# The first FFN of a fused layer in two phases: all up and gate tiles first, their product kept in DRAM, then the down projection in two halves

## The chip, the cores and the metric

One Trainium2 chip, one of its cores. The metric is the device time of one execution of the whole kernel in microseconds (us), median of several runs.

## The reference, cut to what matters

The layer works on 256 latent tokens and 256 context tokens of 2048 features, in float32. The context tokens go through the first FFN only as far as the mixer needs them.

```
def swiglu(u, w_in, w_out):                    # w_in 2048 x 11264, w_out 5632 x 2048
    gate, up = jnp.split(u @ w_in, 2, axis=-1)
    return (jax.nn.silu(gate) * up) @ w_out

ml = (jax.nn.silu(c) @ w_ada + b_ada).reshape(B, 9, D)       # modulation of the latents, 9 rows of 2048
mc = (jax.nn.silu(c_ctx)[None] @ w_ada + b_ada).reshape(1, 9, D)
h  = h  + 0.5 * ml[:, 2] * swiglu(modulate(rmsnorm(h,  g0), ml[:, 0], ml[:, 1]), ffn_w_in[0], ffn_w_out[0])
hc = hc + 0.5 * mc[:, 2] * swiglu(modulate(rmsnorm(hc, g0), mc[:, 0], mc[:, 1]), ffn_w_in[0], ffn_w_out[0])
# then: w_in projection of both streams, pooling and gated DeltaNet heads, w_out,
# a second FFN for the latents alone (ml[:, 6..8]), a final RMSNorm
```

## The kernel before, in words

Activations are held transposed, features on the 128 partitions and 512 tokens (both streams) along the free axis. Every float32 product is made of three matmuls (`product`, L744 to L748): each operand is split into a high part, rounded to the PE's fp32r format, and a low part, the remainder. A **weight tile** is 128 x 1024 floats. SyncE loads it into one of four `raw` buffers, ScalarE (ACT) casts it to its high part `wh` (L1419), VectorE (DVE) subtracts to get the low part `wl` (L1834), and TensorE (PE) uses it in 24 matmuls of 512 tokens. `wh` and `wl` are rings of four. ACT's cast of tile t waits on `tile_used`, until the PE is done with tile t-4. The split runs `AHEAD` = 3 tiles ahead of the PE, in program order: at step x of a group both ACT and DVE split tile x+3.

The first FFN is 11 groups of 512 hidden features. A group is 24 tiles (steps 0 to 23): 16 of up and gate weights (`UP_TILES`, two pairs of 8; each pair fills four PSUM banks) and 8 of the down projection. After the 8th and the 16th tile comes `hidden`: ACT applies silu to two banks (L1478), DVE multiplies (L2028), ACT casts to `hth` (L1481), DVE makes `htl` (L2032). The down projection of the group's four 128-row blocks follows at once, four output columns at a time, and DVE's `gate_out` multiplies it by the modulation gate and adds it to `h_lat` and `h_ctx` (L2050). Groups 0 and 1 are written out by hand: both groups' up tiles, then both groups' down tiles.

The modulation rows (silu(c) and silu(c_ctx) times `w_ada`) are made in two ways. Rows 0 and 1 (shift and scale) are made by the PE at the start. Row 2, the gates of this FFN, is made by the PE too, in 32 quarters (`gate_t`, L754, with L764) between the up tiles of groups 0 and 1. Rows 3 to 8 are made by DVE in **pieces** while the PE does the FFN. A piece has 16 items: ACT issues the load of 128 rows of `w_ada` into `abuf` (two buffers; 1024 columns in the first four pieces, 2048 in the last four; L1466 and L1470), and DVE multiplies them by the vector and adds them to `acc` (L2007, two instructions of 1024 columns for an item in both kinds). ACT's load of item i waits on `acc_done` until DVE has finished item i-2:

```
def load_piece(r, s, i, width):
    act.wait_ge(acc_done, steps(r, s, i - 1))
...
if width and 3 <= j < 3 + KT:            # ACT, step j, after the split of that step
    load_piece(r, s, j - 3, width)
...
if width and 5 <= j < 5 + KT:            # DVE, step j, after the split of that step
    piece(r, s, j - 5, width)
```

So both engines do a split and then the piece's part of that step, in the steps 3 to 18 (ACT) and 5 to 20 (DVE) of groups 2 to 9. The sums over the partitions are made by the PE in the next group (`reduce_rows`, L813, after its second tile, and `reduce_columns`, L820, after its fourth), eight times in all.

Of the kernel before, what the change touches and what calls it, by code (L numbers as in the profile page):

```python
# [11 lines left out]
ds = bass.ds  # L12
# [34 lines left out]
ADA_GATE = KT // 2  # L47
ADA_RING = 8
GATE_RING = 3
# [6 lines left out]
MOD_COLS = (N_MOD - 3) * KT  # L56
# [10 lines left out]
PIECE_FROM = 2  # L67
PIECE_BOTH = 4
PIECE_ONE = 4
LAST = GROUPS - 1  # L70
assert PIECE_FROM + PIECE_BOTH + PIECE_ONE == LAST

T_FFN1 = 0
T_HEADS = T_FFN1 + GROUPS * GROUP_TILES
# [3 lines left out]
T_END = T_FFN2 + GROUPS * GROUP_TILES  # L78


def transfers(t):

    if t < 2 * GROUP_TILES:
        return TILE_K if t < 2 * UP_TILES else 1
    if T_HEADS <= t < T_POOL:
        return TILE_K
    base = T_FFN1 if t < T_HEADS else T_FFN2
    inside = base <= t and (t - base) % GROUP_TILES < UP_TILES
    return TILE_K if inside else 1
# [4 lines left out]


GATE_HOOKS = ((2, 2, 2, 2, 2, 2, 0, 0), (2, 2, 2, 2, 2, 2, 0, 0), (0, 2, 2, 2, 2, 0, 0, 0))


def gate_steps():
    quarters, sums, m = [], [], 0  # L100
    for row in GATE_HOOKS:
        for n in row:
            done = [q // ADA_Q for q in quarters[-1] if q % ADA_Q == ADA_Q - 1] if quarters else []
            sums.append(done)
            quarters.append(list(range(m, m + n)))
            m += n
    assert m == ADA_GATE * ADA_Q
    return quarters, sums


GATE_QUARTERS, GATE_SUMS = gate_steps()
# [73 lines left out]
def laid_out(given):  # L185
# [4 lines left out]
    def columns(a):  # L190
# [5 lines left out]
    w = given["w_ada"][0, :, :3 * D].reshape(KT, P, 3, KT, P)  # L196
    first = w[:, :, 0:2].transpose(3, 0, 1, 2, 4).reshape(ADA_SS, KT, P, ADA_W)
    gate = w[:, :, 2].reshape(KT, P, ADA_GATE, ADA_W).transpose(2, 0, 1, 3)
    ada = np.concatenate([first, gate]).reshape(ADA_SS + ADA_GATE, ADA_Q, KT // ADA_Q, P, ADA_W)
    out = {"xT": features(given["x"]), "ctxT": features(given["ctx"]),  # L200
           "cols": np.ascontiguousarray(np.concatenate(cols + [host["tail"]], axis=1)),
           "ada": np.ascontiguousarray(ada.transpose(0, 1, 3, 2, 4).reshape(
               ADA_SS + ADA_GATE, ADA_Q, P, -1)),
# [12 lines left out]
def build(nc, xT, ctxT, cols_in, ada_in_w, masks_in, pools_in, w_out_t, w_ada, w_in, a_log, dt_bias,  # L216
# [11 lines left out]
    d_xp = scratch("d_xp", (HEADS, NBLK, 8, BLK, BLK))  # L228

    es = ExitStack()  # L230
    with es:  # L231
# [51 lines left out]
        with ExitStack() as st:  # L283
# [10 lines left out]
            with ExitStack() as first:  # L294
                ada_t = sb("ada_t", [P, ADA_RING, KT // ADA_Q, ADA_W], stack=first)
                gate_t = sb("gate_t", [P, GATE_RING, KT // ADA_Q, ADA_W], stack=first)
            with ExitStack() as later:
                sb("apart", [P, KT], stack=later)
                hth2 = sb("hth2", [P, GROUP_FF, SEQ], F32R, stack=later)
                htl2 = sb("htl2", [P, GROUP_FF, SEQ], F32R, stack=later)  # L300
            hth = sb("hth", [P, GROUP_FF, NTOK], F32R, stack=st)
            htl = sb("htl", [P, GROUP_FF, NTOK], F32R, stack=st)
            with ExitStack() as second:
                hth1 = sb("hth1", [P, GROUP_FF, NTOK], F32R, stack=second)
                htl1 = sb("htl1", [P, GROUP_FF, NTOK], F32R, stack=second)
            with ExitStack() as third:
                wba = sb("wba", [P, KT, N_BA], stack=third)
                wbah = sb("wbah", [P, KT, N_BA], F32R, stack=third)
                wbal = sb("wbal", [P, KT, N_BA], F32R, stack=third)
# [70 lines left out]
        gate_in = [sem(f"gate_in{i}") for i in range(GATE_RING)]  # L380
# [84 lines left out]
        STAT_BANK, RB_BANK = 5, (6, 7)  # L465
# [23 lines left out]
        def late_gates(k, s):  # L489

            return gates(0, 0, LAST, 0) + (2 * k + s + 1 if k < LATE else 2 * LATE + s * (KT - LATE) + k - LATE + 1)
# [5 lines left out]
        def steps(r, s, i):  # L497

            return r * (2 * KT) + ((s - PIECE_FROM) * 2 * KT + 2 * i + 4)

# [6 lines left out]
        def _(sp):  # L507
# [3 lines left out]
            for i in range(3):  # L511
                sp.sem_inc(gated[i], PER_DOWN[i])
# [31 lines left out]
            def first_load(t):  # L544
                if t < 2 * UP_TILES:
                    g, j = divmod(t, UP_TILES)
                    load(0, 0, t, up_source(0, 0, g, *divmod(j, K_TILES)))
                else:
                    g, j = divmod(t - 2 * UP_TILES, N_OUT * OUT_TILES)
                    load(0, 0, t, down_source(0, 0, g, *divmod(j, OUT_TILES)))  # L550
# [9 lines left out]
            def gate_load(m):  # L560
                if m >= GATE_RING:
                    sp.wait_ge(ada_used, ADA_SS * ADA_Q + m - GATE_RING + 1)
                sp.dma_start(gate_t[:, m % GATE_RING].rearrange("p k n -> p (k n)"),
                             ada_in_w[ADA_SS + m // ADA_Q, m % ADA_Q]).then_inc(gate_in[m % GATE_RING], 16)

            for i in range(ADA_SS):
                ada_load(i)
                if i >= 3:
                    first_load(i - 3)
            for t in range(13, 2 * GROUP_TILES):  # L570
                first_load(t)
                if t - 13 < len(GATE_QUARTERS):
                    for m in GATE_QUARTERS[t - 13]:
                        gate_load(m)
            with sp.Fori(0, GROUPS - 2) as r:
                group_loads(0, r, 2, 2 * GROUP_TILES)
# [164 lines left out]
        def _(pe):  # L741
            mm, turn = nc.tensor.matmul, nc.tensor.transpose

            def product(out, ah, al, bh, bl, first, last):  # L744

                mm(out, ah, bh, start=first, stop=False)  # L746
                mm(out, ah, bl, start=False, stop=False)  # L747
                return mm(out, al, bh, start=False, stop=last)  # L748
# [59 lines left out]
            def reduce_rows():  # L808


                for c_ in range(4):
                    s, half = divmod(c_, 2)
                    i = mm(ps[32 * c_:32 * (c_ + 1), 7, :], ones.broadcast_to([P, 32]),  # L813
                           acc[:, s, half * TILE_N:(half + 1) * TILE_N], start=True, stop=True)
                i.then_inc(red_pe, 1)

            def reduce_columns():

                for b in range(4):
                    i = mm(ps[:, 7, b:16:4], rsum[:, b * P:(b + 1) * P], sel4, start=True, stop=True)  # L820
# [10 lines left out]
            def up_tile(f, r, t, p, k, x_base=None):  # L831

                pe.wait_ge(lo_done, tiles(r, GROUP_TILES, t) + RAW)
# [36 lines left out]
            def last_block(t):  # L870


                def part(q, kk, bank, x_):
                    k, a = divmod(kk, TILE_K)
                    w = slice(a * TILE_N + q * P, a * TILE_N + (q + 1) * P)
                    return product(ps[:, bank, 0:SEQ], wh[:, (t + k) % HL, w], wl[:, (t + k) % HL, w],
                                   hth[:, kk, x_], htl[:, kk, x_], kk == 0, kk == GROUP_FF - 1)

                pe.wait_ge(lo_done, tiles(0, GROUP_TILES, t + OUT_TILES - 1) + RAW)
                for q in range(4):  # L880
                    for kk in range(GROUP_FF):
                        i = part(q, kk, 4 + q, slice(0, SEQ))
                    i.then_inc(down_done[0], 1)
                pe.wait_ge(gated[0], gates(0, 0, LAST, 3))
                for q in range(4):
                    for kk in range(GROUP_FF):
                        i = part(q, kk, CTX_BANK[q], slice(SEQ, NTOK))
                        if q == 3 and kk % TILE_K == TILE_K - 1:
                            i.then_inc(tile_used, 1)
                    if q < 3:  # L890
                        i.then_inc(down_done[0], 1)
                    if q == 0:
                        stream_sums(0)
                    elif q == 1:
                        stream_rms(0)

            def first_groups():
# [27 lines left out]
                for pair in range(1, 2 * PAIRS):  # L925
                    free = 0 if pair % 2 else 4
                    if pair == 1:
                        pe.wait_ge(cols_set, ADA_SS)
                    else:
                        pe.wait_ge(F[0]["hf_done"], 2 * (pair - 1))  # L930
                        pe.wait_ge(cols_set, ADA_SS + 3 * (pair - 1))
                    for k in range(K_TILES):
                        up_tile(0, 0, pair * K_TILES + k, pair % 2, k)
                        hook = (pair - 1) * K_TILES + k
                        for m in GATE_QUARTERS[hook]:
                            j, q = divmod(m, ADA_Q)
                            if q == 0:
                                pe.wait_ge(F[0]["hf_done"], 2 * pair)
                                pe.wait_ge(arow_set, ADA_SS + j - 1)
# [1713 lines left out]
```

## Time and profile before

| | |
|---|---|
| median of 3 runs | 2919.83 us (2917.42 to 2921.59) |
| span of the profiled execution, first to last instruction | 2915.5 us |
| the profiled execution's own time | not listed apart; the runs' median is 4.3 us above the span |
| PE busy (matmuls) | 2855.9 us, 98% |
| DVE busy | 1687.6 us, 58% |
| ACT busy | 968.1 us, 33% |
| mean DMA rate | 186 GB/s |

A busy share is that of the whole span. Matmuls overlap each other in the records, so the mean duration of one is not its cost; the distance from one start to the next is. The first FFN lies between 65 and 1578 us, the heads and the mixer up to about 2150, the second FFN after that.

### The profile page before, as it was taken

How to read it: one execution, taken by the hardware profiler on the slowest of the kernel's cores; microseconds unless marked ns; L12 is line 12 of the kernel's file. 1: busy time of each engine (PE TensorE's matmuls, PEld its weight loads, DVE VectorE, ACT ScalarE, POOL GpSimd, SP SyncE). 2: the span in 40 equal slices, each digit the busy share in tenths (PEclk: the TensorE clock that was granted, in tenths of full speed). 3: DMA queues.
4: the chain of work that ended last, by engine and by line, in shares of the span. 5: the costliest groups of instructions: out<-in, count | busy, mean ns of one | idle time of the engine just before them, and what ended most of it. 6: DMA issues, size and time to landing. Idle time of an engine off the chain costs nothing. (4 is left out here: it accounts for less than half of the span.)

```text
span 2915.5 us, 47677 instructions
## 1 busy us (share of the span) xinstructions
PE 2855.9 (98%) x18096; PEld 2492.1 (85%) x18096; DVE 1687.6 (58%) x2472; ACT 968.1 (33%) x1443; POOL 238.5 (8%) x388
## 2 busy tenths in 40 slices
PE   6999999999999999999999999999999999999998
PEld 3677888888888888888888888878999999999998
DVE  2522547475665757575726766755675555555555
ACT  2212222222222222222224555544353344344444
POOL 3000000000000000000002013545120000000001
PEclk9999999999999999999999999999999999999999
DMA  9865245555455857567632566685556666566664
GB/s 362 295 208 168 88 144 173 153 155 169 144 173 155 269 185 254 193 224 231 196 98 77 153 194 188 196 260 173 159 178 190 187 184 184 180 186 187 187 187 144
DMA packets 399198, 541.70 MB, mean 186 GB/s; under 512 B 51040, under 2 KB 301920, under 8 KB 390384
## 3 DMA queue, kind: packets, MB, share of 16 engines
q1 hardware_dynamic: 377408, 434.20, 48.4%
q10 hardware_dynamic: 21680, 106.03, 11.1%
q8 instruction: 70, 1.15, 0.2%
q14 instruction: 40, 0.33, 0.0%
HBM read 518.08 MB, written 22.05 MB: 185 GB/s over the span
## 5 line engine op out<-in xcount | busy, mean ns | idle before, releaser
L1834 DVE TENSOR_TENSOR wl<-raw,wh 128x1024 fp32r<-128x1024 f32 x640 | 782.5, 1232 | 722.7 <-ACT wh L1419 721.0
L1419 ACT CAST wh<-raw 128x1024 fp32r<-128x1024 f32 x640 | 666.1, 1047 | 1506.2 <-PE ps L748 1142.5
L746 PE MATMUL ps<-xh,wh 128*128 128x512 f32 (+1 forms) x1920 | 729.8, 380 | 3.2 <-DVE xl L1894 2.5
L747 PE MATMUL ps<-xl,wh 128*128 128x512 f32 (+1 forms) x1920 | 722.2, 376 | 0.0
L748 PE MATMUL ps<-xh,wl 128*128 128x512 f32 (+1 forms) x1920 | 721.5, 376 | 0.0
L748 PE MATMUL ps<-hth,wl 128*128 128x256 f32 (+1 forms) x1424 | 473.8, 333 | 0.0
L746 PE MATMUL ps<-hth,wh 128*128 128x256 f32 (+1 forms) x1424 | 473.3, 332 | 0.0
L747 PE MATMUL ps<-htl,wh 128*128 128x256 f32 (+1 forms) x1424 | 473.1, 332 | 0.0
L746 PEld LDWEIGHTS ps<-xh,wh 128*128 128x128 f32 x1920 | 361.6, 188 | 80.9 <-issue 11.2
L748 PEld LDWEIGHTS ps<-xh,wl 128*128 128x128 f32 x1920 | 361.3, 188 | 67.3
L747 PEld LDWEIGHTS ps<-xl,wh 128*128 128x128 f32 x1920 | 361.7, 188 | 64.9
L746 PE MATMUL ps<-x2h,wh 128*128 128x256 f32 x1408 | 393.8, 280 | 1.7 <-DVE x2l L1894 1.7
L748 PE MATMUL ps<-x2h,wl 128*128 128x256 f32 x1408 | 395.0, 281 | 0.0
L747 PE MATMUL ps<-x2l,wh 128*128 128x256 f32 x1408 | 393.6, 280 | 0.0
L2007 DVE SCALAR_TENSOR_TENSOR acc<-abuf,cT,acc 128x1024 f32<-128x1024 f32 x240 | 297.1, 1280 | 0.2 <-DMA abuf<-in_w_ada 0.2
L747 PEld LDWEIGHTS ps<-htl,wh 128*128 128x128 f32 x1424 | 267.6, 188 | 26.7
L748 PEld LDWEIGHTS ps<-hth,wl 128*128 128x128 f32 x1424 | 267.4, 188 | 26.9
L746 PEld LDWEIGHTS ps<-hth,wh 128*128 128x128 f32 x1424 | 266.9, 187 | 27.3
L746 PEld LDWEIGHTS ps<-x2h,wh 128*128 128x128 f32 x1408 | 264.2, 188 | 2.0 <-issue 2.0
L747 PEld LDWEIGHTS ps<-x2l,wh 128*128 128x128 f32 x1408 | 265.6, 189 | 0.0
L748 PEld LDWEIGHTS ps<-x2h,wl 128*128 128x128 f32 x1408 | 265.1, 188 | 0.0
L2480 POOL TENSOR_TENSOR nacc<-hf 128x512 f32<-128x512 f32 (+1 forms) x4 | 5.4, 1359 | 2232.3 <-ACT hf L1509 1486.9
(264 smaller groups left out, 2287.8 us busy)
## 6 DMA issues: line engine op xcount, KB each, us to landing
raw<-in_ffn_w_in SPq DMA_DIRECT2D x704, 256.0 KB, 3.3
raw<-in_ffn_w_out SPq DMA_DIRECT2D x176, 512.0 KB, 4.1
abuf<-in_w_ada ACTq DMA_DIRECT2D x64, 1024.0 KB, 5.8
ada_t<-in_ada SPq DMA_DIRECT2D x64, 512.0 KB, 9.3
abuf<-in_w_ada ACTq DMA_DIRECT2D x64, 512.0 KB, 3.8
raw<-in_w_in SPq DMA_DIRECT2D x128, 256.0 KB, 3.7
gate_t<-in_ada SPq DMA_DIRECT2D x32, 512.0 KB, 5.0
raw<-in_w_out SPq DMA_DIRECT2D x32, 512.0 KB, 4.6
```

The source lines that it names most:

```text
L746: mm(out, ah, bh, start=first, stop=False)
L747: mm(out, ah, bl, start=False, stop=False)
L748: return mm(out, al, bh, start=False, stop=last)
L1419: nc.scalar.copy(wh[:, t % HL, :], raw[:, t % RAW, :]).then_inc(hi_done, 1)
L1834: tt(wl[:, t % HL, :], raw[:, t % RAW, :], wh[:, t % HL, :].bitcast(F32), ALU.subtract).then_inc(lo_done, 1)
L2007: n = stt(acc[:, b, :], src, c_, acc[:, b, :], ALU.mult, ALU.add)
L2480: i = tt(nacc[:, x_], sq[:, 0, x_], sq[:, 1, x_], ALU.add)
```

## The change

The first FFN becomes two phases. In the **up phase** all 11 groups of 16 up and gate tiles follow one another (`up_pairs`). The product of each pair, high and low part, is written to a DRAM tensor `d_h` by two DMAs of ACT (`hidden_out`), at step 10 of the same group for the first pair and at step 2 of the next for the second. The last group's four blocks stay in SBUF. In the **down phase** the output is made in two halves of 1024 features. A half runs over all 44 blocks, one weight tile of 128 x 1024 for each, into all eight PSUM banks, and adds to `h_lat` and `h_ctx` once at its end. ACT loads the blocks from 5 on back (`hidden_in`, 512 KB each) into the upper rows of `xl`. A half is closed bank by bank over its last tiles: 2 in the first half, 4 in the second, whose last four output blocks are closed for the latents and then the context, as before.

The gates (row 2) are no longer made by the PE's quarters. They are two further pieces, so there are 10: six of 1024 columns for both streams, then four of 2048. Item i of a piece is loaded at step i+10 of its group or step i-6 of the next, and worked on by DVE at step i+12 or i-4. The sums are made by the PE after tile 11 and after tile 13 of the next group.

```diff
-PIECE_BOTH = 4
-PIECE_ONE = 4
+PIECE_BOTH = 3 * D // HALF                       # 6
+PIECE_ONE = (N_MOD - 5) * D // (2 * HALF)        # 4
+PIECE_AT = 12
+LOAD_AT = PIECE_AT - 2
+K_FF = D_FF // P                                 # 44
+HELD = 2 * PAIRS                                 # 4
+SPILLED = GROUPS * PAIRS - PAIRS
+HALF_TILES = K_FF
+CLOSE = 2
+CLOSE_LAST = 4
+HR = 4
...
# TensorE
-            def reduce_rows():
+            def reduce_rows(r, n):
+                pe.wait_ge(acc_done, steps(r, n, KT))
+                pe.wait_ge(F[0]["hf_done"], r * GROUP_FF + ((n + 1) * GROUP_FF + 2))
...
-                        for m in GATE_QUARTERS[hook]:
-                            j, q = divmod(m, ADA_Q)
...
-                            ada_quarter(q, free + j % 2, gate_t[:, m % GATE_RING],
-                                        gate_in[m % GATE_RING], 16 * (m // GATE_RING + 1))
-                        for j in GATE_SUMS[hook]:
-                            ada_columns(ADA_SS + j, free + 2)
...
+            def up_pairs(r, m):
+                for x in range(UP_TILES):
+                    p, k = divmod(x, K_TILES)
+                    if k == 0:
+                        pe.wait_ge(F[0]["hf_done"], r * GROUP_FF + (m * GROUP_FF + 2 * p - 2))
+                        if p == 0 and m >= 2:
+                            pe.wait_ge(red_out, r * 2 + 2 * (m - 1))
+                    up_tile(0, r, m * UP_TILES + x, p, k)
+                    if x == PIECE_AT - 1:
+                        reduce_rows(r, m - 1)
+                    elif x == PIECE_AT + 1:
+                        reduce_columns(r, m - 1)
...
+            def down():
...
+                for a, close in enumerate((CLOSE, CLOSE_LAST)):
+                    for i in range(HELD):
+                        ff_tile(0, a, i)
+                    with pe.Fori(0, (HALF_TILES - HELD) // HR - 1) as r:
+                        for b in range(HR):
+                            ff_tile(r, a, HELD + b)
+                    for i in range(HALF_TILES - HR, HALF_TILES - close):
+                        ff_tile(0, a, i)
+                    closing_tiles = range(HALF_TILES - close, HALF_TILES)
+                    for i in closing_tiles:
+                        ff_arrived(0, a, i)
+                    for c in range(8 if a == 0 else 4):
+                        ff_whole(a, c, closing_tiles)
...
# ScalarE
+            def up_pairs(r, m, before=None):
+                for x in range(UP_TILES):
...
+                    split(r, UP_TILES, m * UP_TILES + x + AHEAD)
+                    if x < LOAD_AT and m:
+                        load_piece(r, m - 1, x + KT - LOAD_AT)
+                    elif x >= LOAD_AT and m < GROUPS - 1:
+                        load_piece(r, m, x - LOAD_AT)
+                    if x == 2 and m:
+                        hidden_out(r, m, -1)
+                    elif x == K_TILES + 2 and m < GROUPS - 1:
+                        hidden_out(r, m, 0)
+                    if x % K_TILES == K_TILES - 1:
...
+                        hidden(0, r, m, tiles(r, UP_TILES, m * UP_TILES + x), p, hth)
+
+            def down_tile(r, a, i, spread=True):
+                split(r, HR, T_DOWN + a * HALF_TILES + i + AHEAD)
+                if HELD <= i + AHEAD and spread:
+                    hidden_in(r, a, i + AHEAD)
...
# VectorE
+            def up_pairs(r, m):
+                for x in range(UP_TILES):
+                    if m or x >= K_TILES - 1:
+                        split(r, UP_TILES, m * UP_TILES + x + AHEAD)
+                    if m and x == PIECE_AT:
+                        reduced_rows(r, m - 1)
+                    elif m and x == PIECE_AT + 2:
+                        reduced(r, m - 1)
+                    if x < PIECE_AT and m:
+                        piece(r, m - 1, x + KT - PIECE_AT)
+                    elif x >= PIECE_AT and m < GROUPS - 1:
+                        piece(r, m, x - PIECE_AT)
+                    if x % K_TILES == K_TILES - 1:
+                        hidden(0, r, m, x // K_TILES, hth, htl)
```

Two places show how instructions move. The first is ACT at the start of a group of the loop over the wide pieces. Before, it holds splits alone up to step 3:

```order
L1418 ISA
L1419 CAST wh<-raw 128x1024
L1417 REGISTER_ALU
L1418 REGISTER_ALU
L1419 CAST wh<-raw 128x1024
L1418 REGISTER_ALU
L1419 CAST wh<-raw 128x1024
L1418 REGISTER_ALU
L1419 CAST wh<-raw 128x1024
L1463 ISA
L1470 ISA
L1470 DMA abuf<-in_w_ada 128x2048
```

The same place after the change, from the group's third split on:

```order
L1455 CAST wh<-raw 128x1024
L1500 REGISTER_ALU
L1506 ISA
L1506 DMA abuf<-in_w_ada 128x2048
L1531 ISA
L1534 ISA
L1534 DMA d_h<-hth 128x2x512
L1534 ISA
L1534 DMA d_h<-htl 128x2x512
L1454 REGISTER_ALU
L1455 CAST wh<-raw 128x1024
```

Each split is now followed by the load of an item, in every step, and in step 2 (and 10) by the two stores of a pair as well.

The second is the PE at the first sum of a piece. Before, it stands after two tiles of the group, whose predecessor's items ended at step 20:

```order
L748 MATMUL ps<-xh,wl 128x512
L964 REGISTER_ALU
L965 REGISTER_ALU
L813 MATMUL ps<-acc,cols 32x512 x4
L833 REGISTER_ALU
L746 MATMUL ps<-xh,wh 128x512
```

After the change it stands between tile 11 and tile 12 of the group, and DVE's last item of that piece is at step 11:

```order
L758 MATMUL ps<-xh,wh 128x512
L759 MATMUL ps<-xl,wh 128x512
L760 MATMUL ps<-xh,wl 128x512
L826 MATMUL ps<-acc,cols 32x512 x4
L758 MATMUL ps<-xh,wh 128x512
```

The sum moved from five steps behind the last item to the end of the tile in whose time the last item is worked on.

## Rows read from the trace of the kernel before

**Rows 1.** The page: busy time, and the span in 40 slices (tenths)

```profile
PE 2855.9 (98%) x18096; PEld 2492.1 (85%) x18096; DVE 1687.6 (58%) x2472; ACT 968.1 (33%) x1443; POOL 238.5 (8%) x388
...
PE   6999999999999999999999999999999999999998
...
PEclk9999999999999999999999999999999999999999
```

**Rows 2.** Groups: count | busy us, mean ns | idle before, releasers

```profile
L746 PE MATMUL ps<-xh,wh 128*128 128x512 f32 (+1 forms) x1920 | 729.8, 380 | 3.2 <-DVE xl L1894 2.5
```

**Rows 3.** Windows of PE: length, busy (instructions), granted clock, DMA share, GB/s

```profile
131.84:294.94 163.10, 163.10 (x906) 1.00 0.58 187
...
381.98:469.02 87.04, 87.04 (x386) 1.00 0.57 169
512.54:601.75 89.21, 89.21 (x401) 1.00 0.56 165
```

**Rows 4.** Windows of all engines (PE, PEld, DVE, ACT, POOL), steps 8 to 14

```profile
1089.00:1127.00 38.00, 38.00 (x169) 31.49 (x168) 26.25 (x24) 9.55 (x11) 0.00 (x0) 1.00 0.84 279
```

**Rows 5.** Timeline of PE, then ACT: start, duration, steps 6 to 8

```profile
1083.78 0.39 PE L746 MATMUL ps<-xh,wh 128*128 128x512 f32 x1
...
1078.54 1.05 ACT L1419 CAST wh<-raw 128x1024 fp32r<-128x1024 f32 x1 [4.39 <-PE ps L748]
...
1083.98 1.05 ACT L1419 CAST wh<-raw 128x1024 fp32r<-128x1024 f32 x1 [4.39 <-PE ps L748]
...
1089.42 1.09 ACT L1478 ACTIVATE sg<-ps 128x512 f32<-128x512 f32 x2 [4.39 <-PE ps L748]
1090.77 1.22 ACT L1481 CAST hth<-hf 128x512 fp32r<-128x512 f32 x2 [0.27 <-DVE hf L2028]
1091.89 1.04 ACT L1419 CAST wh<-raw 128x1024 fp32r<-128x1024 f32 x1
```

**Rows 6.** Timeline of ACT, then DVE, steps 10 and 11

```profile
1102.13 0.34 ACTq L1470 DMA_DIRECT2D abuf<-in_w_ada  x1
1102.60 1.05 ACT L1419 CAST wh<-raw 128x1024 fp32r<-128x1024 f32 x1 [4.28 <-DVE acc L2007]
1107.45 0.34 ACTq L1470 DMA_DIRECT2D abuf<-in_w_ada  x1
1107.92 1.05 ACT L1419 CAST wh<-raw 128x1024 fp32r<-128x1024 f32 x1 [4.27 <-DVE acc L2007]
...
1103.68 1.22 DVE L1834 TENSOR_TENSOR wl<-raw,wh 128x1024 fp32r<-128x1024 f32 x1 [1.71 <-ACT wh L1419]
1104.82 2.47 DVE L2007 SCALAR_TENSOR_TENSOR acc<-abuf,cT,acc 128x1024 f32<-128x1024 f32 x2
```

**Rows 7.** Timeline of ACT, steps 15 and 16

```profile
1129.27 1.05 ACT L1419 CAST wh<-raw 128x1024 fp32r<-128x1024 f32 x1 [4.27 <-DVE acc L2007]
...
1134.59 1.09 ACT L1478 ACTIVATE sg<-ps 128x512 f32<-128x512 f32 x2 [4.27 <-DVE acc L2007]
...
1137.07 1.04 ACT L1419 CAST wh<-raw 128x1024 fp32r<-128x1024 f32 x1
```

**Rows 8.** Lines L1466 (512 KB) and L1470 (1 MB): from issue to landing

```profile
DMA to landing us min/median/max: 3.5/3.8/5.1
...
DMA to landing us min/median/max: 4.7/5.8/8.4
```

**Rows 9.** Timeline of PE around two stretches of lower clock, and one as window

```profile
1951.20 0.63 PE L1200 MATMUL ps<-GI,UF 32*32 32x32 f32 x16 [3.04 <-DMA UF<-d_uf]
...
1951.00:1961.00 10.00, 9.74 (x118) 0.50 1.05 383
...
126.78 0.77 PE L746 MATMUL ps<-xh,wh 128*128 128x512 f32 x1
...
131.62 0.39 PE L748 MATMUL ps<-xh,wl 128*128 128x512 f32 x1
```

More of the change, by code:

```diff
@@ L55 @@
 PB = HALF // P
-MOD_COLS = (N_MOD - 3) * KT
+MOD_COLS = (N_MOD - 2) * KT
+M_GATE, M_SHIFT1, M_SCALE1, M_GATE1, M_SHIFT2, M_SCALE2, M_GATE2 = (KT * i for i in range(N_MOD - 2))
 GROUP_FF = 4
@@ L78 @@
 T_END = T_FFN2 + GROUPS * GROUP_TILES
+SPARE = (T_HEADS, T_HEADS + 1)
 def transfers(t):
-    if t < 2 * GROUP_TILES:
-        return TILE_K if t < 2 * UP_TILES else 1
-    if T_HEADS <= t < T_POOL:
-        return TILE_K
-    base = T_FFN1 if t < T_HEADS else T_FFN2
-    inside = base <= t and (t - base) % GROUP_TILES < UP_TILES
+    if t < T_DOWN:
+        return TILE_K
+    if t < T_HEADS:
+        return 1
+    if t < T_POOL:
+        return TILE_K
+    inside = T_FFN2 <= t and (t - T_FFN2) % GROUP_TILES < UP_TILES
     return TILE_K if inside else 1
 FIRST_TILES = {6: 0, 7: 1, 8: 2, 9: 3, 11: 4, 13: 5, 15: 6}
[L96 to L111, printed above, removed]
 SCAN = ((2, 3, 0, 1), (3, 2, 1, 0))
@@ L510, in _ @@
             sp.sem_inc(tile_used, HL)
-            for i in range(3):
+            for i in range(1, 3):
                 sp.sem_inc(gated[i], PER_DOWN[i])
@@ L742, in _, with product @@
             mm, turn = nc.tensor.matmul, nc.tensor.transpose
[L744 to L748, printed above, removed]
+            def product(out, ah, al, bh, bl, first, last, reopened=False):
+                mm(out, ah, bh, start=first, stop=False, skip_group_check=reopened)
+                mm(out, ah, bl, start=False, stop=False, skip_group_check=reopened)
+                return mm(out, al, bh, start=False, stop=last, skip_group_check=reopened)
             def ada_quarter(q, bank, buf, arrived, count):
@@ L868, in down_block, with ff_part @@
                             mark(part(q, kk), q, kk)
[L870 to L892, printed above, removed]
+            def ff_part(a, i, c, x_, last=False, reopened=False):
+                t = T_DOWN + a * HALF_TILES + i
+                w = slice(c * P, (c + 1) * P)
+                bh, bl = held(i) if i < HELD else fetched(i)
+                return product(ps[:, down_bank(a, c), x_], wh[:, t % HL, w], wl[:, t % HL, w], bh[:, x_], bl[:, x_],
+                               i == 0, last, reopened)
@@ new lines, in hidden_out, with hidden_in @@
+            def hidden_out(r, m, p):
+                n, b = 2 * m + p, 2 * (p % 2)
+                act.wait_ge(F[0]["h_ready"], r * GROUP_FF + 2 * (n + 1))
+                rows = slice(2 * n, 2 * n + 2) if isinstance(r, int) else ds(r * GROUP_FF + 2 * n, 2)
+                for part, src in enumerate((hth, htl)):
+                    act.dma_start(d_h[rows, :, part, :].rearrange("b p n -> p b n"), src[:, b:b + 2, :].bitcast(F32)
+                                  ).then_inc(hid_out, 16)
+            def hidden_in(r, a, i):
+                rows = slice(i - HELD, i - HELD + 1) if isinstance(r, int) else ds(r * HR + i - HELD, 1)
+                at_ = 8 + 2 * (i % HR)
+                act.dma_start(xl[:, at_:at_ + 2, :].bitcast(F32), d_h[rows].rearrange("b p s n -> p (b s) n")
+                              ).then_inc(hid_in[i % HR], 16)
@@ L1747, in _, with first_high @@
                 split(0, 0, t)
-            for t in range(2 * GROUP_TILES):
-                if t < K_TILES:
-                    high(0, 2 * t)
-                    high(0, 2 * t + 1)
-                split(0, 0, t + AHEAD)
-                if t < 2 * UP_TILES and t % K_TILES == K_TILES - 1:
-                    g, p = divmod(t // K_TILES, PAIRS)
-                    hidden(0, 0, g, t + 1, p, (hth, hth1)[g])
-            with act.Fori(0, PIECE_BOTH) as r:
-                group(0, r, PIECE_FROM, PIECE_FROM * GROUP_TILES, width=1)
-            with act.Fori(0, PIECE_ONE) as r:
-                s = PIECE_FROM + PIECE_BOTH
-                group(0, r, s, s * GROUP_TILES, width=2)
-            group(0, 0, LAST, LAST * GROUP_TILES, closing=last_squares, early=decay_weights, left=1)
+            def first_high(x):
+                if x < K_TILES:
+                    high(0, 2 * x)
+                    high(0, 2 * x + 1)
+            up_pairs(0, 0, first_high)
+            with act.Fori(0, PIECE_BOTH - 1) as r:
+                up_pairs(r, 1)
+            up_pairs(0, PIECE_BOTH)
+            with act.Fori(0, PIECE_ONE - 1) as r:
+                up_pairs(r, PIECE_BOTH + 1)
+            up_pairs(0, GROUPS - 1)
+            down()
             square_stream(LATE, 1)
```

398 lines of the change are left out of this document (214 added, 184 removed).

## Prediction

> **What bounds the kernel now.** I read the page first [rows 1]: the PE is busy for 98% of the span, slice after slice of the first FFN is full and its clock stays high there. The groups of instructions give the same for the PE's idle time: ahead of the FFN tiles' first matmul form there are 3.2 us in 1920 instructions [rows 2]. So the time is now what the PE's program costs, and work of other engines is free as long as it is in time. The windows give the PE's prices [rows 3]. Sixteen up tiles of a group without a sum take 87.04 us, 5.44 us for a tile. With one piece's two sums among them they take 89.21, so the two sums of a piece cost 2.17 us. The stretch with the PE's quarters of row 2 is 163.10 us long.
>
> Next I read who works beside the PE while a piece is made. Between 1089 and 1127 us DVE is busy for 26.25 of 38 us and ACT for 9.55 [rows 4]; by share neither is near its limit. The timelines show another thing. ACT's cast starts 0.20 us after the PE's tile starts (1083.78, 1083.98) when it is on time [rows 5]. With an item in each step it is not the PE that releases ACT but DVE: the idle time before the cast ends with "DVE acc L2007" [rows 6]. Cast, subtraction, the item's two instructions, the issue of the next load: cast to cast is 1102.60 to 1107.92, 5.32 us. The PE's step is 5.44, so a delayed chain gains only 0.12 us in a step. The item of a step ends at 1104.82 + 2.47 = 1107.29, that is 4.69 us after its cast began.
>
> **What is removed.** The 163.10 us hold 612 product matmuls of the FFN, 25.5 tiles, 138.7 us at 5.44. The rest is 24.4; a column sum of another row within it, about 0.4, stays. Gates: **-24.0 us**. The FFN's products themselves are the same in number (24 matmuls for each of 264 tiles).
>
> **What is added on the PE.** Two more pieces are summed: 2 x 2.17 = **+4.3 us**.
>
> **The wait at the first sum.** The PE's first sum now stands behind tile 11 and needs item 15, which DVE works on in step 11, in the time of that very tile. Before, items ended at step 20 and the sum came five steps later, so a delay of the chain reached nobody. Now the margin is what is left of one tile: 5.44 - 0.20 - 4.69 = 0.55 us when the chain is on time. It is not on time. One passage of `hidden` takes ACT from cast to cast 1083.98 to 1091.89, 7.91 us, so it costs 2.47 over a tile [rows 5]; inside a late chain 1129.27 to 1137.07, 7.80, so 2.36 [rows 7]. Both passages of a group (steps 15 and 7) now lie between one sum and the next with an item in every step; before, eight or so steps of a group had no item, in which the delay was paid back. Then `hidden_out`: two stores in step 2 and two in step 10, issued by ACT right between the load and the next cast. An issue shifts ACT's next cast by 0.47 us (1102.13 to 1102.60) [rows 6], four of them 1.88. About ten steps pay back 0.12 each, 1.2. The delay at step 11 is 2.47 + 2.36 + 1.88 - 1.2 = 5.5 us; less the margin, the PE waits 5.0 us in a group. DVE's two copies of sums are paid by the PE's own 2.17 us beside them. Nine groups make 45; in the last group the stores of step 10 and the loads after it are missing, so some 2.2. **+47.2 us.** The bounds: without the stores in the chain it is 3.1 a group, about 28 in all; if an issue that stands behind another DMA took twice as long, about 64.
>
> The Trainium skill ("DMA: Bandwidth & Descriptors", section "Issuing engines are not separate DMA queues") says that the time an engine's sequencer takes to initiate a DMA is usually small beside the DMA itself. The trace agrees on the size, 0.47 us against landings of 3.8 and 5.8 us [rows 6, 8]. By that rule one would price the stores at nothing and get about 19 us less.
>
> **The clock after the wait.** The PE has not stood still in this FFN so far, so the price comes from two other places [rows 9]. After a wait of 3.04 us the stretch from 1951 to 1961 ran at a granted clock of 0.50, the lower level, 1.2 GHz. From 126.78 to 131.62, after short waits of about 0.6 us among light matmuls, eleven starts took 4.84 us, where 11 x 0.2267 = 2.49 is the full pace: 2.3 us lost. I take 2.3 us for each of ten waits, **+23 us**. Bounds: nothing, if the clock stays up through 5 us of standing still, and about 4 us for a wait (+40), if the lower level holds as in the first of the two places.
>
> **The DMA beside the wide pieces.** Steps 8 to 14 of a wide piece already have the DMA engines busy for 0.84 of the time at 279 GB/s [rows 4]; in proportion, 332 GB/s is the full rate. A group with a wide piece now moves 16 x 0.5 MB of weights, 16 x 1 MB of `w_ada` and 1 MB of stores with both parts, 27.3 million bytes. Over 87.04 + 2.17 + 5.0 = 94.2 us that is 290 GB/s, 0.87: it fits on average. But a load of `abuf` is issued when the item two before is done and is wanted about 7.7 us later, and such a load lands after 4.7 to 8.4 us, median 5.8 [rows 8]. Late ones delay the chain that already ends the PE's wait. I put 1 us for each of four groups, **+4 us**; bounds 0 and 3 us a group.
>
> **The down phase.** In a tile of 5.44 us ACT casts for 1.05 and issues one load, DVE subtracts for 1.23 [rows 6]: no chain comes near. `hidden_in` is issued three tiles ahead, some 14 us, and 512 KB land after 3.8 us, at most 5.1 [rows 8]. Closing the first half over two tiles gives DVE one bank per six matmuls, 1.36 us, for an addition of 512 columns; an item's 2 x 1024 columns take it 2.47 [rows 6], so I estimate a bank at some 0.7 us and this closing at nothing (bounds 0 and 3 us, were each bank late by a third). In the second half the last four tiles are held until all four are there, and there are only four `wh`: the cast and the load of block 43 start when tile 39 has been used. That is 0.2 for ACT's start, 0.2 for issues and 3.8 for the landing [rows 8], **+4.0 us**, and another 2.3 for the clock. These two are **+6.3**. If tile 43's block were issued earlier than the cast, this falls to about nothing; if its load lands late, 5.6.
>
> **The sum.** -24.0 + 4.3 + 47.2 + 23 + 4 + 6.3 = +60.8. On the profiled execution's span of 2915.5 this gives 2976.3; the median is 4.3 us above the span, so 2980.6, rounded to **2980 us**.
>
> **The rivals.** A: *the PE's sum decides, no wait.* Spoken for by the shares in [rows 4], where DVE has a third of its time free; against it stands the cast-to-cast distance of 5.32 in [rows 6]. The time would be -24.0 + 4.3 + 4 = -15.7, so 2904. It decides if the wait at the first sum stays under about 1 us a group with the clock up, that is, if the chain runs at some 4.9 us a step so that passages are paid back in five steps. This is the other sign: faster. Chance 0.07. The Trainium skill ("Perfetto Trace Analysis", section "Identifying the Most-Contended Engine") tells one to find the limiting engine by occupancy; by it DVE is no limit and the PE's own work decides. That row agrees on the shares, and the rule leaves out the order in which the items must come.
>
> B: *the same wait at the lower size.* The stores' issues lie outside the chain (28 instead of 47.2), and the clock stays up or nearly: -24.0 + 4.3 + 28 + 4 + 4 = +16.3, 2936; with a third of the clock's price, 2944. For it: the clock's price comes from places with lighter matmuls before the wait. Chance 0.12.
>
> C: *the wide pieces become DMA-bound.* Every item's 1 MB lands late because the stores share the queues with loads at 0.84 busy. With 20 to 30 us more for the four wide groups the time is 3005 to 3015 and above. Against it: the rate needed, 290 GB/s, lies below 332. Chance 0.06.
>
> My forecast has the remaining 0.75.
>
> **How the numbers follow.** The likeliest case alone reaches from 2951 (no clock price, nothing for the DMA: 60.8 - 25.3 - 4 = +31.5) to 3005 (12 for the DMA, 17 more for the clock: +85.8, rounded). Eight times in ten the range should hold the time; it takes in the upper half of B, and the lower part of C: 2938 to 3010. A measurement of this kernel can tell about 0.2%, 6 us, from no change. Faster by more than that: rival A and a rest of other mishaps in my prices, 0.08. Within: 0.02, since it would need the waits to sum to just the gates' 20 us. Slower: 0.90.
>
> **What would show it.** In the changed kernel the PE's timeline has, in front of the sum's matmuls behind tile 11 of each group from the second on, an idle time of 4 to 6 us ended by DVE's `acc`, ten in all; a group period near 96 us instead of 89.2; a granted clock below 1 in the window behind that sum and near 1 elsewhere; no such gap in the down phase until the last four tiles, where one of some 4 us is ended by a cast or by a landing. ACT's casts in the up phase are released by DVE's items from step to step. It would be wrong if those gaps are under 1 us (A), if the gaps are 3 us and the clock doesn't fall (B), or if DVE's items wait for a DMA (C).

## The result, and the profile after

The changed kernel takes 2977.14 us (median of 4 runs, 2968.99 to 2980.93) against 2918.62 us for the kernel before (4 runs, 2913.81 to 2921.59). The ratio is 1.0201, 95% interval 1.018 to 1.0221: slower by 58.5 us. The forecast was 2980 and slower. Single runs of one kernel spread by some 10 us, and part of that lies where no edit of this document reaches: from the sums of the norm ahead of it to those of the last norm, the second FFN lasts 745.1 and 745.3 us in the traces of experiments 3 and 4 and 754.0 to 754.5 us in the other nine.

The page of the kernel after answers to [rows 1]: the PE has 256 matmuls fewer and DVE is less busy than before, ACT is where it was, yet the PE's share fell from 98 to 96%. The slices show hardly more (one dip in the first FFN, one later): waits of 6 us are too short for slices of 74. The mean clock stands in the row of the core, 0.977; the trace of the kernel before has 0.994, and the kernel of experiment 1 below, which has hardly any of the waits, 0.989.

```profile
PE 2858.0 (96%) x17840; PEld 2496.2 (84%) x17840; DVE 1633.4 (55%) x2197; ACT 968.1 (33%) x1443; POOL 237.9 (8%) x388
...
PE   6999999999998999999999999998999999999998
```

```profile
core 0: 2978.0 us, clock 0.977
```

So the page says "less work, and slower". The timeline of the PE shows where the time is. This is the sum behind tile 11 of the fifth group (start, duration, engine, line, operation, idle time before it and what ended it):

```profile
539.89 0.39 PE L760 MATMUL ps<-xh,wl 128*128 128x512 f32 x1
546.17 1.93 PE L826 MATMUL ps<-acc,cols 128*32 128x512 f32 x8 [5.89 <-DVE acc L2092]
```

There are ten such waits, as forecast, of 6.05, 5.90, 5.91, 5.89, 5.89, 3.41, 6.78, 7.45, 5.82 and 3.14 us. The windows put a price on one group (length, PE busy, granted clock, DMA share, GB/s): from sum to sum in the narrow pieces, in the sixth, in a wide piece, then the wait alone and the 9.83 us behind it.

```profile
448.28:546.17 97.89, 92.00 (x401) 0.95 0.63 193
642.95:738.28 95.33, 91.92 (x401) 0.97 0.64 194
837.08:936.67 99.59, 92.14 (x400) 0.95 0.81 274
540.27:546.17 5.90, 0.01 (x2) 0.72 0.93 292
546.17:556.00 9.83, 9.83 (x40) 0.82 0.68 212
```

A group took 89.21 us of the PE before [rows 3]; the first one shown takes 97.89. The chain ahead of the wait is to be read on ACT, which answers to [rows 5 to 7]: two steps, one with the stores.

```profile
529.55 1.05 ACT L1455 CAST wh<-raw 128x1024 fp32r<-128x1024 f32 x1 [4.33 <-PE ps L760]
534.41 0.34 ACTq L1503 DMA_DIRECT2D abuf<-in_w_ada  x1
534.87 1.05 ACT L1455 CAST wh<-raw 128x1024 fp32r<-128x1024 f32 x1 [4.27 <-PE ps L760]
539.73 0.34 ACTq L1503 DMA_DIRECT2D abuf<-in_w_ada  x1
540.24 0.41 ACTq L1534 DMA_DIRECT2D d_h<-hth  x1
540.81 0.41 ACTq L1534 DMA_DIRECT2D d_h<-htl  x1
541.34 1.04 ACT L1455 CAST wh<-raw 128x1024 fp32r<-128x1024 f32 x1 [5.42 <-issue]
```

529.55 to 534.87 is 5.32, the step forecast. 534.87 to 541.34 is 6.47: the two stores shift the next cast by 1.15 us. (The releaser "PE ps L760" is the row's inference for a cast that follows a load; the load at 534.41 comes 0.17 us behind DVE's item, which ends at 534.24.) The last wait of the down phase is there too:

```profile
1608.89 0.39 PE L760 MATMUL ps<-xl,wl 128*128 128x512 f32 x1
1612.87 0.76 PE L758 MATMUL ps<-xl,wh 128*128 128x512 f32 x1 [3.59 <-DVE el L1929]
```

### The profile page after: what moved, and what is told of

Read it like the earlier page. It is cut to its first block and busy times, and to the rows that moved or that the text cites. A ratio compares the mean times of both kernels' runs of the same rounds, so it can differ in the third digit from the quotient of the medians.

```text
span 2978.0 us, 47625 instructions
## 1 busy us (share of the span) xinstructions
PE 2858.0 (96%) x17840; PEld 2496.2 (84%) x17840; DVE 1633.4 (55%) x2197; ACT 968.1 (33%) x1443; POOL 237.9 (8%) x388
## 5 line engine op out<-in xcount | busy, mean ns | idle before, releaser
L759 PE MATMUL ps<-xl,wh 128*128 128x512 f32 (+1 forms) x2560 | 973.8, 380 | 0.0
L760 PE MATMUL ps<-xh,wl 128*128 128x512 f32 (+1 forms) x1904 | 720.8, 379 | 0.0
L759 PEld LDWEIGHTS ps<-xl,wh 128*128 128x128 f32 x2560 | 485.9, 190 | 90.8
L760 PEld LDWEIGHTS ps<-xh,wl 128*128 128x128 f32 x1904 | 361.2, 190 | 67.4
L760 PE MATMUL ps<-x2h,wl 128*128 128x256 f32 x1408 | 393.8, 280 | 0.0
L2092 DVE SCALAR_TENSOR_TENSOR acc<-abuf,cT,acc 128x1024 f32<-128x1024 f32 x300 | 371.2, 1278 | 4.4 <-DMA abuf<-in_w_ada 4.2
L760 PEld LDWEIGHTS ps<-x2h,wl 128*128 128x128 f32 x1408 | 265.7, 189 | 0.0
L758 PE MATMUL ps<-xl,wh 128*128 128x512 f32 (+1 forms) x656 | 253.0, 386 | 3.6 <-DVE el L1929 3.6
L760 PE MATMUL ps<-xl,wl 128*128 128x512 f32 (+1 forms) x656 | 252.7, 385 | 0.0
L759 PE MATMUL ps<-htl,wh 128*128 128x256 f32 (+1 forms) x768 | 222.7, 290 | 0.0
L760 PE MATMUL ps<-hth,wl 128*128 128x256 f32 (+1 forms) x768 | 222.7, 290 | 0.0
L758 PE MATMUL ps<-hth,wh 128*128 128x256 f32 (+1 forms) x768 | 222.7, 290 | 0.0
L760 PEld LDWEIGHTS ps<-hth,wl 128*128 128x128 f32 x768 | 147.1, 192 | 2.5
```

The source lines that it names most:

```text
L758: mm(out, ah, bh, start=first, stop=False, skip_group_check=reopened)
L759: mm(out, ah, bl, start=False, stop=False, skip_group_check=reopened)
L760: return mm(out, al, bh, start=False, stop=last, skip_group_check=reopened)
L2092: m = stt(acc[:, b, :], src, c_, acc[:, b, :], ALU.mult, ALU.add)
```

## The experiments

My theory: the closed chain of cast, subtraction, item and issue is late by two passages of `hidden` and four issues, the PE waits for the last item, and the clock falls. The rivals: DVE's own work is the limit; issues cost nothing; the clock's loss has another cause. All ratios are against the kernel before, whose medians in these sessions were 2916.38 to 2918.62 us.

**1. The load one step later.**

```diff
-LOAD_AT = PIECE_AT - 2
+LOAD_AT = PIECE_AT - 1
```

> ACT's load of an item stands one step later in its program (LOAD_AT = PIECE_AT - 1): its wait is then on an item that DVE did a step ago, so ACT's cast no longer waits for the item of the same step. Nothing else changes; DVE's work, its order and the PE's sum behind tile 11 stay. Theory (the delay comes from the closed chain cast, subtraction, item, issue): DVE alone needs 1.23 + 2.47 = 3.7 us of 5.44, pays a passage of hidden back in two steps and is on time at step 11; the ten waits (57 us after the change) fall to under 1 us each and with them the clock's loss (some 23 us): about 2897 us. Rival (DVE's own work is too much, or the item in the same step is by itself too late): the waits stay at 3 us or more, 2940 to 2977. Second rival (the load, asked for 0.8 us later, lands late in the four wide pieces): waits gone in the first six groups and still 3 to 7 us in three or four of the wide ones, about 2920 to 2935.

Measured: 2899.82 us, ratio 0.993 (0.9903 to 0.9957). One number gives 77 us back. The same stretch of ACT and of the PE (ACT's cast is now released by the PE in almost every step, the load comes 0.2 us behind it, the stores lie in ACT's idle time; and the sum stands right behind its tile):

```profile
504.91 1.05 ACT L1455 CAST wh<-raw 128x1024 fp32r<-128x1024 f32 x1 [4.39 <-PE ps L760]
505.12 0.34 ACTq L1503 DMA_DIRECT2D abuf<-in_w_ada  x1
505.63 0.41 ACTq L1534 DMA_DIRECT2D d_h<-hth  x1
506.20 0.41 ACTq L1534 DMA_DIRECT2D d_h<-htl  x1
510.35 1.05 ACT L1455 CAST wh<-raw 128x1024 fp32r<-128x1024 f32 x1 [4.39 <-PE ps L760]
```

```profile
515.37 0.39 PE L760 MATMUL ps<-xh,wl 128*128 128x512 f32 x1
515.68 1.06 PE L826 MATMUL ps<-acc,cols 128*32 128x512 f32 x8
```

```profile
426.50:515.68 89.18, 89.18 (x401) 1.00 0.69 212
784.28:874.26 89.98, 89.25 (x400) 1.00 0.88 305
```

The narrow groups are at 89.18 us with a clock of 1.00, the PE's sum and nothing else. DVE does exactly the work it did. The rival "DVE is too slow" is out. Three wide groups keep 0.6 to 1.1 us.

**2. The stores on SyncE.**

```diff
 # SyncE, up phase
     for x in range(UP_TILES):
         up_load(r, 1, x)
+        if x in (2, K_TILES + 2):
+            n, b = x // K_TILES, 2 * (x // K_TILES)
+            sp.wait_ge(F[0]["h_ready"], r * GROUP_FF + 2 * (n + 1))
+            for part, src in enumerate((hth, htl)):
+                sp.dma_start(d_h[...], src[:, b:b + 2, :]).then_inc(hid_out, 16)
 # ScalarE
-                    if x == 2 and m:
-                        hidden_out(r, m, -1)
-                    elif x == K_TILES + 2 and m < GROUPS - 1:
-                        hidden_out(r, m, 0)
```

> The four stores of a group are issued by SyncE among its weight loads, behind the loads of tiles 2 and 10, in place of ACT. Theory (each pair of issues on ACT shifts the next cast by 1.15 us, as in the trace after the change, and nothing pays it back): the wait at the sum falls by about 2.3 us a group, from 5.9 to 3.6, some 20 us less in all, and the clock's loss stays, since a wait of over 3 us remains: about 2957 us. Rival (issues cost nothing, as their own time is small beside the transfer): within 5 us of 2977. Rival (SyncE's wait for htl holds up the weights): new waits on lo_done in front of tiles, slower than 2977.

Measured: 2950.95 us, ratio 1.0098 (1.0072 to 1.0124), 26 us less than with the stores on ACT. The waits of the first five groups are 3.31 to 3.37 us, the sixth is 1.35:

```profile
535.55 0.64 PE L832 MATMUL ps<-acc,cols 128*32 128x512 f32 x4 [3.35 <-DVE acc L2094]
```

```profile
441.61:535.55 93.94, 90.59 (x400) 0.98 0.67 201
```

The ten waits sum to 34.0 us where they were 56.9 (each counted from start to start, less the 0.32 of a sum that doesn't wait): 2.3 us a group, as forecast. The clock was not to change and did: the nine periods between the ten sums last 848.15 us; less 9 x 89.18 and the 30.6 of waits in them, 14.9 is left, 1.7 for a wait, where the changed kernel has 2.4 (worked out below). Waits and clock together are a little more than the 26 us. No idle time appears in front of a tile of the up phase, so the rival that SyncE holds up the weights falls.

**3. The wait filled with matmuls.**

```diff
 def reduce_rows(r, n):
-    pe.wait_ge(acc_done, steps(r, n, KT))
     pe.wait_ge(F[0]["hf_done"], r * GROUP_FF + ((n + 1) * GROUP_FF + 2))
+    for _ in range(12 if n in (PIECE_BOTH - 1, PIECES - 1) else 24):
+        mm(ps[:, RED_BANK, :], xh[:, 0, 0:P], xl[:, 0, :], start=True, stop=True)
+    pe.wait_ge(acc_done, steps(r, n, KT))
```

> The PE runs matmuls that nobody needs (24 of 128x128 by 512 into the sum's bank, 12 in the last narrow and the last wide piece) in front of its wait for the item, in the time in which it would stand still. The item's time doesn't change. Theory (a wait of 6 us costs 6 us and then some 2.3 us more, because the clock falls to its lower level): the sum starts when it did, the granted clock stays at 1.00 around it, and the group's period falls from 97.4 to about 95: some 20 to 23 us less, about 2955. Rival (the clock's loss has another cause than the standing still, or the sum's own matmuls bring it): the clock window behind the sum stays at 0.68 and the time within 5 us of 2977.

Measured: 2957.23 us, ratio 1.0143 (1.0124 to 1.0162), 20 us less for 240 matmuls more. (The case with 12 never applies, since one loop body of the PE serves all groups from the third on; in the sixth and the last group the 24 take about 2 us more than the wait was.) From the first norm's sums to the next norm's the trace is 18.9 us shorter than that of the changed kernel. The 24 fill the wait but for 0.38 us, the sum begins no earlier, and behind it the clock is 1.00, where it was 0.82 in a window of about that length:

```profile
531.03 5.60 PE L824 MATMUL ps<-xl,xh 128*128 128x512 f32 x24
537.01 1.06 PE L828 MATMUL ps<-acc,cols 128*32 128x512 f32 x8 [0.38 <-DVE acc L2094]
```

```profile
441.94:537.01 95.07, 94.69 (x424) 1.00 0.66 199
537.01:547.00 9.99, 9.99 (x47) 1.00 0.71 211
```

The period is 95.07: 89.18, and 5.9 for the item that isn't there yet. The clock's part was real, and it comes from standing still.

**4. The second half closed over three tiles.**

```diff
-CLOSE_LAST = 4
+CLOSE_LAST = 3
```

> The second half is closed over its last 3 tiles instead of 4 (CLOSE_LAST = 3). Theory (block 43's load and cast can only start when tile 39 has been used, and with four tiles held the PE has nothing else to do until they are there): with tile 40 worked on in the usual way the wait of 3.59 us and the clock's 2.3 us behind it vanish, 5 to 6 us less, about 2972; up to 2 us of it may come back in the end, where the norm has less work of the PE beside it. Rival (the wait is the landing alone and moves to tile 43 as it is): same time as after the change, 2977.

Measured: 2971.99 us, ratio 1.0174 (1.0147 to 1.0201), 5 us less, which is within the spread of the runs. The trace tells more. The same window of the PE, in the changed kernel and in this one:

```profile
1600.00:1614.00 14.00, 10.41 (x44) 0.90 0.63 200
```

```profile
1600.00:1614.00 14.00, 14.00 (x63) 1.00 0.67 193
```

No idle time of 0.8 us or more is left in the down phase. From the last sum of a piece to the first matmul of the norm's sums it is 1128.66 to 1631.23, 502.57 us, against 1128.35 to 1633.48, 505.13. These 2.6 us understate the gain: behind the last sum this trace has a granted clock of 0.72 over 9.83 us and loses 2.55 us in the next 100 matmuls, while the changed kernel's has 1.00 there and loses nothing. Without that the down phase is 5.1 us shorter. The norm's part behind it is 2.2 us longer (580.71 against 578.54 to the next norm). So the wait is gone with its clock, and about 2 of the 5 us come back.

**5 and 6. The edits together.**

> The two edits that took a wait away together: the load of an item one step later in ACT's program, and the second half closed over three tiles. By the theory they act in different places and add up: no wait over 1.5 us in the whole first FFN, 2899.8 - 5 = about 2895 us, against 2918.2 before. Rival: they don't add up, since the closing's gain in the last runs (5 us) was within the spread of them: 2900.

Measured: 2898.85 us (10 runs), ratio 0.9942 (0.9922 to 0.9961). That is 1 us below experiment 1, so the 5 us of the closing can't be seen in the time, and the forecast of 2895 was some 4 us low. The traces do show them, here without any loss of clock behind the last sum: from that sum to the norm's it is 505.21 us in experiment 1 and 500.02 in this one, and the norm's part behind is 578.29 and 579.06.

> As the last, and the stores issued by SyncE. Theory: the price of 1.15 us for two issues counts only where ACT stands in the closed chain; with the chain opened they lie in ACT's idle time, so moving them off ACT gives nothing: the same as the last run within 3 us, about 2895. Rival (a store costs by itself, chain or not): some 20 us less, 2875.

Measured: 2898.1 us (9 runs), ratio 0.9934 (0.9911 to 0.9956). The same move that was worth 26 us in experiment 2 is worth nothing once the chain is open. All nine periods are 89.18 to 89.34 us. It is the fastest version by the median, but not one that the measurement can tell from experiments 1 and 5.

**7. ACT's loops written out.**

```diff
-            with act.Fori(0, PIECE_BOTH - 1) as r:
-                up_pairs(r, 1)
-            up_pairs(0, PIECE_BOTH)
-            with act.Fori(0, PIECE_ONE - 1) as r:
-                up_pairs(r, PIECE_BOTH + 1)
-            up_pairs(0, GROUPS - 1)
+            for m in range(1, GROUPS):
+                up_pairs(0, m)
```

> The changed kernel with ACT's two loops over the groups of the up phase written out (ten calls with constant numbers in place of registers); every instruction that works is the same and in the same order. In the trace after the change the one narrow group that is written out already has a step of 5.16 us from cast to cast instead of 5.32, without ALU and MOVE instructions between the issue and the cast, and a wait of 3.4 us instead of 5.9. Theory (ACT's register instructions lie in the closed chain and cost 0.16 us a step): all groups' waits fall by about 2.4 us, to 3.4 in the narrow ones and 3.5 to 5 in the wide ones, some 20 us less: about 2956. Rival (that group is short because the loads of the wide piece begin in it, or by chance): the waits stay at 5.9, 2977.

Measured: 2961.26 us, ratio 1.0158 (1.0115 to 1.0201), 16 us less. From cast to cast it is now 586.73 to 591.92 and 591.92 to 597.08, 5.19 and 5.16 us:

```profile
586.73 1.05 ACT L1455 CAST wh<-raw 128x1024 fp32r<-128x1024 f32 x1 [4.14 <-DVE acc L2088]
591.46 0.36 ACTq L1503 DMA_DIRECT2D abuf<-in_w_ada  x1
591.92 1.05 ACT L1455 CAST wh<-raw 128x1024 fp32r<-128x1024 f32 x1 [4.14 <-DVE acc L2088]
596.65 0.34 ACTq L1503 DMA_DIRECT2D abuf<-in_w_ada  x1
597.08 1.05 ACT L1455 CAST wh<-raw 128x1024 fp32r<-128x1024 f32 x1 [4.11 <-DVE acc L2088]
```

The waits of the first five groups are 3.31 to 3.47 us, and the sixth group, which was written out already, stays near what it was (3.73 for 3.41). The register instructions that a loop needs between a wait and the next instruction are part of the chain. All ten waits sum to 37.9 us, 19 less; the clock's loss stays (22.3 us in the nine periods, where it was 21.7), and the time is 5 us above the forecast.

**8. No gate quarters, in the kernel before.**

```diff
-                            ada_quarter(q, free + j % 2, gate_t[:, m % GATE_RING],
-                                        gate_in[m % GATE_RING], 16 * (m // GATE_RING + 1))
+                            pe.wait_ge(gate_in[m % GATE_RING], 16 * (m // GATE_RING + 1))
+                            pe.sem_inc(ada_used, 1)
```

> The kernel before, whose PE leaves out the 32 quarters of the gates (their loads, the rows' copies and the column sums stay, so row 2 is made from what lies in the bank, and the first FFN's gates are other numbers). This measures the removed term alone. Theory (the quarters cost the PE 16.0 us of their own and some 4 us in slower matmuls around them; the column sums' 3.4 us stay): 2918 - 20 = about 2898. Rival (work hidden beside something else): under 5 us.

Measured: 2897.9 us (10 runs), ratio 0.9941 (0.9923 to 0.9958), so 12 to 22 us of 2916.38, 17 in the middle, 18.5 by the medians. In the traces the first sum of a piece begins at 504.50 instead of 523.51, 19.0 us earlier:

```profile
504.50 0.64 PE L813 MATMUL ps<-acc,cols 128*32 128x512 f32 x4
```

**9. Half the bytes in the wide pieces.** On top of experiment 1:

```diff
-                    act.dma_start(abuf[:, i % 2].rearrange("p s n -> p (s n)"), src).then_inc(...)
+                    act.dma_start(abuf[:, i % 2, 0, :], src[:, 0:HALF]).then_inc(...)
...
 # VectorE
-                    src = abuf[:, i % 2, 0 if n < PIECE_BOTH else b, :]
+                    src = abuf[:, i % 2, 0, :]
```

> The kernel with the load one step later, whose loads in the four wide pieces bring only 1024 of the 2048 columns (512 KB in place of 1 MB; DVE uses them twice, with the same instructions, so rows 5 to 8 hold other numbers). In the run with the load later three wide groups still had 0.6 to 1.1 us of waiting at the sum (periods of 89.8 to 90.2 instead of 89.18), and DVE's items waited for a DMA 14 times, 13.6 us. Theory (what is left there is the late landing of 1 MB loads): all periods 89.2 us and no item waits for a DMA; 2 to 3 us less, about 2897, which the time alone can't tell. Rival (the rest comes from DVE's chain in those groups): the periods stay at 89.8 to 90.2.

Measured: 2901.18 us, ratio 0.9933 (0.9912 to 0.9953), not to be told from experiment 1 by its time. All nine periods are 89.18 us and no item waits for a DMA. So what the wide groups of experiment 1 still waited for, 2.5 us in all, was the landing of 1 MB; it differs from one execution to the next, for experiment 6, with the whole loads, kept only 0.2. In experiment 1 these loads land after 4.7, median 5.8, at most 10.1 us, here after 3.4, 3.7 and 5.8:

```profile
DMA to landing us min/median/max: 4.7/5.8/10.1
```

```profile
DMA to landing us min/median/max: 3.4/3.7/5.8
```

## Why the prediction was right, step by step

**The gates, -24.0.** The kernel before has its quarters between the start of the 193rd matmul of the up tiles and that of the 768th, which ends the first two groups. This stretch takes 154.2 us there, 134.4 without the quarters (experiment 8), and 132.5 in experiment 1, which has neither quarters nor column sums, but one piece's two sums of 2.17. So the quarters cost 19.8 us and the column sums 4.1, together 23.9: the step holds. (The 19.0 us by which the first sum of a piece moved in experiment 8 are less, since its trace is 0.8 us late before the quarters begin.) Ahead of this stretch the changed kernel's trace gains another 2.1 us, for which the forecast has no term: the lower clock at 126.78 [rows 9] is missing there. That is luck of this execution and not the change, for every experiment's trace but the third has such a stretch again, between 115 and 132 us, and the 193rd matmul of the up tiles starts 91.9 to 97.0 us behind the first norm's first sum, in no order with the edits.

**The wait at the first sum, +47.2.** The mechanism, the place, the number of waits and the releaser were right (5.9 us for 5.0 in the first five groups). The sixth group waited only 3.4, because ACT's program is written out there and a step takes 5.16 us and not 5.32, as experiment 7 shows for the others; the forecast made no difference between them. The sizes: two issues cost 1.15 and not 0.94 (0.4 us a group), and the rest of 0.5 us is spread over the passages and steps. Ten waits sum to 56.9 us, counted from start to start and less the 0.32 that a sum without a wait has. They hold the late loads of the wide pieces too. The sum for both terms was 51.2, and 56.9 came. Rival A falls: the wait was far from 1 us. The shares spoke for it, and on the page after the change none of them is higher than before, yet the PE waits. Experiment 1 is what the rival describes: the same work with the order mended, at 2899.82 us for the rival's 2904.

**The clock, +23.** Nine periods between the ten sums last 875.1 us; less 9 x 89.18 and the nine waits of 50.8 in them, 21.7 is left, 2.4 for a wait. The tenth wait, of 3.14 us, cost nothing: the granted clock behind it is 1.00. Experiment 3 took the loss away. Rival B falls with it.

**The DMA, +4.** The row of DVE's items in the changed kernel has the time that they waited for a load:

```profile
L2092 DVE SCALAR_TENSOR_TENSOR acc<-abuf,cT,acc 128x1024 f32<-128x1024 f32 x300 | 371.2, 1278 | 4.4 <-DMA abuf<-in_w_ada 4.2
```

All of it lies in the wide pieces: 0.8 us ahead of the wait of 6.78, 1.5 ahead of that of 7.45 and 2.1 ahead of the last. The step holds. Experiment 9 shows that the cause was the one named, for what is left of it with the chain open. Rival C, a wide phase limited by the DMA, didn't come: even with the waits gone the wide groups need 305 GB/s and run at 89.2 to 90.2 us a group.

**The closing, +6.3.** The wait was 3.59 us, forecast 4.0. The row names `el` as its releaser, but that is the split of the next phase's first tile, which the PE doesn't need there; tile 43's own split lies one before it on DVE. What the program waits for beside it is block 43, issued on ACT when tile 39 was used; such loads land after 3.3 us in the median:

```profile
1609.39 0.35 ACTq L1541 DMA_DIRECT2D xl<-d_h  x1
```

```profile
DMA to landing us min/median/max: 3.1/3.3/6.2
```

The load issued at 1609.39 landed after 3.3 us, at 1612.73, and the PE goes on at 1612.87, 0.14 us behind. In all six traces that have this wait (the changed kernel and experiments 1, 2, 3, 7 and 9) the distance from this landing to the PE is 0.135 to 0.137 us, while that from the end of the first half of `el` varies from 0.06 to 0.15. No experiment moved the load alone, but this leaves little room for another releaser. With its clock the closing cost 5.1 us (experiments 4 and 5), 1.2 less than forecast.

The sum by measured terms is -23.9 - 2.1 + 4.3 + 56.9 + 21.7 + 5.1 = 62.0. In the traces the first FFN is 61.6 us longer (1588.8 for 1527.2, from the first norm's sums to the next norm's), the spans differ by 62.5, the medians by 58.5. The mechanism was right, but that 2980 lies 3 us from the median is partly luck: the waits were forecast 5.7 us too small, and against that stand the 2.1 us of the start, 1.3 of the clock and 1.2 of the closing; the spread of the runs covers the rest.

Three slips in the working changed nothing in the forecast. Rival C's 20 to 30 us on top of 2980.6 make 3001 to 3011 and not 3005 to 3015. Ten microseconds at a granted clock of 0.50 [rows 9] lose 5 us and not 4, so the upper bound of the clock's term was +50. And the stores of a group are 1 MB for each of the two parts, as its 27.3 million bytes have it.

By the Trainium skill ("DMA: Bandwidth & Descriptors", section "Issuing engines are not separate DMA queues") initiating DMAs on more than one engine saves only the time that this takes on the sequencer. Experiments 2 and 6 agree with that and set its limits: twenty pairs of stores moved gave 26 us where the issuer stood in a closed chain, and nothing where it didn't.

## What to carry to other kernels

Occupancy can't show a closed chain: DVE was busy for 69% and ACT for 25% of a stretch [rows 4] in which both ran one behind the other at 5.32 us of a 5.44 us step. Where two engines wait for each other in every step, take the distance from one start to the next, subtract it from the step of the engine that bounds, and ask how many steps it takes to pay back each thing that comes once (here 2.5 us of `hidden` at 0.12 a step: never within a group). Before moving a consumer closer to such a chain, loosen the chain: one load asked for one step later turned 58 us slower into 18 us faster.

## What was not expected of the hardware

The register instructions of a loop on ACT lie in such a chain: 5.32 us a step with them, 5.16 to 5.19 without, 0.15 us or so that add up to 2.4 us in a group, because the margin was only 0.12 us. The price of the clock is not proportional to the wait. It is read from the 100 matmuls behind a sum, against the 21.09 us that they take at a granted clock of 1.00. Nothing was lost after waits of 0.4 to 1.8 us (experiments 1, 2, 3 and 5), 1.5 us after one of 2.07 (experiment 2), 1.3 to 3.0 after those of 3.3 to 3.8, and 1.6 to 3.0 after those of 5.8 to 6.1, from group to group; yet nothing after the last waits of the changed kernel and of experiment 7, 3.14 and 3.07 us. What decides within these ranges stays open. Two issues one behind the other took 1.15 us of the next cast, where one had cost 0.47.
